# Hybrid decoder step on one core: transposed outputs and norm sums move to the small-work banks, sampled scores go ahead of attention, hosted work starts later

## The reference

```python
u = rmsnorm(h, norm_mix_g);  proj = u @ w_in
oa = banded_attention(...)            # A: window 128, 4 q heads, 2 kv heads, sinks
ob = ssd_chunked(...)                 # B: Mamba-2 scan in 16 chunks of 128
oc = dilated attention                # C: (128,1), (512,4), (2048,16), joined per query
h = h + concat(oa, ob, oc) @ w_out
u2 = rmsnorm(h, norm_mlp_g)
h = h + square(relu(u2 @ w_up)) @ w_down      # w_up 1024 x 4096, w_down 4096 x 1024
```

## Time and profile before

| | |
|---|---|
| median of 3 runs | 2558.17 us (2557.70 to 2562.37) |
| the profiled execution, its own time | 2557.03 us |
| span in its profile | 2554.8 us, 43225 instructions |
| TensorE busy | 2410.4 us, 94% |
| VectorE, ScalarE, GpSimd busy | 48%, 33%, 11% |
| granted TensorE clock, mean | 0.98 of full speed |
| DMA | 414 MB, 162 GB/s |

### The profile page before, as it was taken

How to read it: one execution, slowest core, us unless ns; L and a number is a source line. 1 busy time by engine, 2 the same in 40 slices (tenths; PEclk the granted TensorE clock), 3 DMA queues, 4 the chain that set the end, 5 groups by cost and what they waited for, 6 DMA issues and landing times.

```text
span 2554.8 us, 43225 instructions
## 1 busy us (share of the span) xinstructions
PE 2410.4 (94%) x17509; PEld 1411.2 (55%) x17509; DVE 1234.8 (48%) x2843; ACT 846.2 (33%) x1533; POOL 278.7 (11%) x305
## 2 busy tenths in 40 slices
PE   7899968999888999999899999989999999999999
PEld 4455535555434555444455554445655447788887
DVE  3445446566646767742644654135566521422222
ACT  4444235464435443331433331124432111311210
POOL 0111222111102211001110100011101001000000
PEclk8899989999999999999999999999999999999999
DMA  6454264665574667775434556533455553322232
GB/s 209 166 173 165 100 229 150 215 209 181 177 237 154 213 204 230 246 257 180 154 118 153 153 163 178 159 119 106 156 172 167 159 163 117 96 92 99 93 99 81
DMA packets 327588, 414.44 MB, mean 162 GB/s; under 512 B 62111, under 2 KB 248095, under 8 KB 327136
## 3 DMA queue, kind: packets, MB, share of 16 engines
q1 hardware_dynamic: 327392, 411.69, 50.0%
HBM read 300.00 MB, written 111.62 MB: 161 GB/s over the span
## 4 chain that ended last, share of the span: by engine, by line
PE 74%; DVE 6%; ACT 3%; issue 2%; DMA 1%; SPq 1%; POOL 0%; DVEq 0%; ACTq 0%; POOLq 0%
PE core_dense L2299 64%; PE core_spare L2399 2%; PE core_spare L2413 1%; PE core_spare L2387 1%; PE core_spare L2425 1%; PE core_spare L2553 1%; DVE core_col L2013 1%; DVE core_p L1939 1%; ACT core_p L1715 1%; PE core_spare L2547 1%; PE core_spare L2531 0%; PE core_spare L2539 0%; DVE core_h L1907 0%; PE core_spare L2533 0%; DVE core_r L1895 0%
## 5 line engine op out<-in xcount | busy, mean ns | idle before, releaser
L2299 PE MATMUL core_dense<-core_u,core_ring 128*128 128x512 f16 (+2 forms) x4800 | 870.2, 342 | 22.2 <-ACT core_yt L1688 5.7
L2299 PEld LDWEIGHTS core_dense<-core_u,core_ring 128*128 128x128 f16 x4800 | 469.4, 98 | 396.4 <-issue 41.0
L2299 PE MATMUL core_dense<-core_r_hi,core_ring 128*128 128x512 f16 (+2 forms) x2560 | 649.0, 339 | 2.7 <-DVE core_h L1907 1.5
L2299 PE MATMUL core_dense<-core_r_lo,core_ring 128*128 128x512 f16 (+2 forms) x1280 | 434.0, 339 | 0.0
L2299 PEld LDWEIGHTS core_dense<-core_r_hi,core_ring 128*128 128x128 f16 x2560 | 250.4, 98 | 197.9 <-issue 5.7
L2299 PE MATMUL core_dense<-tok_u,core_ring 128*128 128x512 f16 x1152 | 266.0, 387 | 16.8 <-DMA core_ring<-scratch_kept_w 16.8
L1680 ACT ACTIVATE core_r<-core_dense 128x512 f32<-128x512 f32 (+2 forms) x160 | 82.3, 515 | 528.9 <-PE core_dense L2299 528.9
L1895 DVE TENSOR_TENSOR core_r<-core_r 128x512 f32<-128x512 f32 (+2 forms) x160 | 96.4, 603 | 321.6 <-ACT core_r L1680 321.2
L628 PE MATMUL tok_prod<-tok_w_hi,tok_u 128*128 128x512 f16 (+1 forms) x768 | 200.4, 351 | 0.0
L2299 PEld LDWEIGHTS core_dense<-tok_u,core_ring 128*128 128x128 f16 x1152 | 114.0, 100 | 147.7 <-DMA core_ring<-scratch_kept_w 14.3
L2299 PEld LDWEIGHTS core_dense<-core_r_lo,core_ring 128*128 128x128 f16 x1280 | 125.2, 98 | 93.4 <-issue 0.7
(11 more groups left out here) (309 smaller groups left out, 2704.3 us busy)
## 6 DMA issues: line engine op xcount, KB each, us to landing
core_ring<-scratch_kept_w SPq DMA_DIRECT2D x264, 512.0 KB, 4.3
scratch_kept_w<-core_ring SPq DMA_DIRECT2D x72, 512.0 KB, 5.6
core_qkv<-out_tok SPq DMA_DIRECT2D x48, 384.0 KB, 5.6
core_staged<-in_w_up SPq DMA_DIRECT2D x32, 512.0 KB, 4.7
core_staged<-in_w_down SPq DMA_DIRECT2D x32, 512.0 KB, 4.6
out_tok<-tok_tok SPq DMA_DIRECT2D x16, 644.0 KB, 3.0
core_piece<-in_c_kt SPq DMA_DIRECT2D x32, 288.0 KB, 3.9
core_piece<-in_c_v SPq DMA_DIRECT2D x16, 576.0 KB, 4.6
```

Of the source, the lines that this page charges most:

```text
L2299: ins = pe.matmul(bank, w[:, k, part, :], s, start=first and j == 0, stop=last and j == 2, skip_group_check=True)
```

## The change

Three things are done.

1. `y` and `tail` units leave the dense banks: they take spare4 (i even) and spare5 (i odd). `sum` takes spare2, and spare3 for the second piece of block 3. `out`, `up`, `down` and `col` go on alternating on the two dense banks.
2. `sk` stands ahead of the `att` or `scan` unit of its slot instead of behind it, on every engine. Its banks are spare0 and spare1 in slots with attention (`sk_bank`), spare3 and spare4 behind those; before they were spare5 and spare4 throughout.
3. `HOST_FROM` leaves 1, 1 and 3 slots empty at the start of blocks 0, 1 and 2, and all hosted attention, scan and join work comes that much later. `sq` stays at slot 1 (one attention step earlier in terms of the attention), `split` and `sk` of block 1 stay where they were. In block 2 the `sx` units go from slots 0, 2, 4 to the emptied slots 0, 1, 2, and `split`, `sv`, `se` shift by 3 with the attention.

```diff
@@ -935,6 +935,7 @@
         real_no = list(itertools.accumulate((int(t[3]) for t in att), initial=0))
         kind0_no = list(itertools.accumulate((int(t[3] and t[0] == 0) for t in att), initial=0))
         BIAS_SLOT = (0, 1, 2, 0)
+        HOST_FROM = (1, 1, 3)
         OUT_AFTER = ((), (), (0, 1), (2, 3), (4, 5), (6, 7), (), ())
 
         def att_slots(first, end):
@@ -990,7 +991,7 @@
             for b in range(NB):
                 beside = iter(())
                 if b + 1 < NB:
-                    some = [[s] for s in att_slots(att_end[b + 1], att_end[b + 2])]
+                    some = [[] for _ in range(HOST_FROM[b])] + [[s] for s in att_slots(att_end[b + 1], att_end[b + 2])]
                     for c in range(4 * b + 4, 4 * b + 8):
                         x1, x2, x3 = scan_parts(c)
                         some += [[x1], [], [x2], [x3]]
@@ -1001,14 +1002,14 @@
                         some[1] = some[1] + [("sq", 0, 0, 0)]
                         for k in range(16):
                             some[3 + 3 * k] = some[3 + 3 * k] + [("split", k, 0, 0)]
-                            some[5 + 3 * k] = some[5 + 3 * k] + [("sk", k // 2, k % 2, 0)]
+                            some[5 + 3 * k] = [("sk", k // 2, k % 2, 0)] + some[5 + 3 * k]
                     if b == 2:
                         for k in range(3):
-                            some[2 * k] = some[2 * k] + [("sx", k, 0, 0)]
+                            some[k] = some[k] + [("sx", k, 0, 0)]
                         for k in range(16):
-                            some[8 + 2 * k] = some[8 + 2 * k] + [("split", 16 + k, 0, 0)]
-                            some[9 + 2 * k] = some[9 + 2 * k] + [("sv", k // 2, k % 2, 0)]
-                        some[41] = some[41] + [("se", 0, 0, 0)]
+                            some[11 + 2 * k] = some[11 + 2 * k] + [("split", 16 + k, 0, 0)]
+                            some[12 + 2 * k] = some[12 + 2 * k] + [("sv", k // 2, k % 2, 0)]
+                        some[44] = some[44] + [("se", 0, 0, 0)]
                     beside = iter(some)
                 for q in range(4):
                     for f in range(HF):
@@ -1045,6 +1046,10 @@
         order, bank_of, need, last_use = {}, {}, {}, {}
         counts = collections.Counter()
 
+        def sk_bank(n, j, s):
+
+            return (0 if 5 + 3 * (2 * n + j) < att_end[2 + 1] - att_end[2] + 4 else 3) + s
+
         def claim(key, bank, sem, n):
             if bank in last_use:
                 need.setdefault(key, []).append(last_use[bank])
@@ -1063,16 +1068,21 @@
             if kind in ("out", "sum", "up", "down", "y", "tail"):
                 for q, _, _ in pieces(b) if kind in ("out", "sum", "up", "down") else [(0, 0, 0)]:
                     order[kind, b, i, q] = counts[kind]
-                    bank = counts["dense"] % NDENSE
-                    bank_of[kind, b, i, q] = dense[bank]
                     counts[kind] += 1
-                    counts["dense"] += 1
                     if kind in ("y", "tail"):
                         counts["act" if i % 2 else "dve"] += 1
                         free = (y_act, counts["act"]) if i % 2 else (y_dve, counts["dve"])
                     else:
                         free = ({"out": out_added, "sum": total_log, "up": r_ready, "down": down_added}[kind], counts[kind])
-                    claim((kind, b, i, q), f"dense{bank}", *free)
+                    if kind in ("y", "tail", "sum"):
+                        bank = 2 + q if kind == "sum" else 4 + i % 2
+                        bank_of[kind, b, i, q] = spare[bank]
+                        claim((kind, b, i, q), bank, *free)
+                    else:
+                        bank = counts["dense"] % NDENSE
+                        bank_of[kind, b, i, q] = dense[bank]
+                        counts["dense"] += 1
+                        claim((kind, b, i, q), f"dense{bank}", *free)
                 if kind in ("out", "up", "down"):
                     slot_free.append(({"out": out_done, "up": up_done, "down": down_done}[kind], counts[kind]))
             elif kind == "dt" and b:
@@ -1121,8 +1131,8 @@
             elif kind == "sq":
                 claim(("SQ",), 5, smp_step, LOW_Q)
             elif kind == "sk":
-                for bank in (4, 5):
-                    claim(("SK", b, i), bank, smp_taken, 2 * b + i + 1)
+                for s in range(2):
+                    claim(("SK", b, i), sk_bank(b, i, s), smp_taken, 2 * b + i + 1)
             elif kind == "sx" and b == 0:
                 for bank in (0, 1):
                     claim(("SN",), bank, smp_step, SCORED)
@@ -2212,9 +2222,9 @@
                         dve.wait_ge(smp_done, 2 * n + j + 1)
                         for s in range(2):
                             if j == 0:
-                                dve.tensor_copy(st[:, 2 * s:2 * s + 2, now], spare[5 - s][:, 12:20].rearrange("p (q t) -> p q t", t=DEC_T))
+                                dve.tensor_copy(st[:, 2 * s:2 * s + 2, now], spare[sk_bank(n, j, s)][:, 12:20].rearrange("p (q t) -> p q t", t=DEC_T))
                             last = dve.tensor_copy(st.rearrange("p (k h) t -> p k h t", h=4)[:, 1:4, 2 * j + s, now],
-                                                   spare[5 - s][:, 0:12].rearrange("p (k t) -> p k t", t=DEC_T))
+                                                   spare[sk_bank(n, j, s)][:, 0:12].rearrange("p (k t) -> p k t", t=DEC_T))
                         last.then_inc(smp_taken, 1)
                     elif kind == "sx":
                         softmax(n)
@@ -2571,7 +2581,7 @@
                                 for s in range(2):
                                     rows = slice(HD * s, HD * s + HD)
                                     at = 12 + DEC_T * q
-                                    both(spare[5 - s][:, at:at + DEC_T], lambda l: halves[rows, l, KC * P:], lambda l: qs[rows, l, q, DEC_T * n:DEC_T * n + DEC_T])
+                                    both(spare[sk_bank(n, j, s)][:, at:at + DEC_T], lambda l: halves[rows, l, KC * P:], lambda l: qs[rows, l, q, DEC_T * n:DEC_T * n + DEC_T])
                         for k in range(KC):
                             t0, w = (0, DEC_T) if k == 0 else ((k - 1) % 4, 1)
                             row = 0 if k == 0 else 1 + (k - 1) // 4
@@ -2579,7 +2589,7 @@
                                 rows = slice(HD * s, HD * s + HD)
                                 at = row * DEC_T + t0
                                 q0 = DEC_T * n + t0
-                                last = both(spare[5 - s][:, at:at + w], lambda l: halves[rows, l, k * P:(k + 1) * P], lambda l: qs[rows, l, 2 + j, q0:q0 + w])
+                                last = both(spare[sk_bank(n, j, s)][:, at:at + w], lambda l: halves[rows, l, k * P:(k + 1) * P], lambda l: qs[rows, l, 2 + j, q0:q0 + w])
                         last.then_inc(smp_done, 1)
                     elif kind == "sx" and n == 0:
                         free(pe, "SN")
```

## The result

The changed kernel takes 2517.48 us (median of four runs, 2510.2 to 2521.22) against 2558.49 us before: ratio 0.983, 95% interval 0.981 to 0.986. That is 41 us less where 34.7 were forecast. The time lies in the prediction's whole range of 2516 to 2536. In five more runs it took 2515.28 us, ratio 0.984 (0.982 to 0.986). The profiled execution took 2519.41 us, its span is 2517.3 us.

The account below looks back on a forecast made before the run. TensorE, busy 2410.4 of 2554.8 us, bounds the kernel; only its idle and lower-clock time can shrink. Gains of 10.3 + 15.6 + 8.8 = 34.7 us give a median of 2523.4 us, own range 2518 to 2529, whole range 2516 to 2536.

Parts of the forecast that it names:

- All 7.8 us go: Dense tiles behind `y`, hand-overs and end of block 3: all 21 waits for DVE's draining vanish, 7.8 us gained.
- the 1.05 of the sums: Three `sum` matmuls, each waiting 0.35 us for a dense bank: waits vanish on the new banks, 1.05 us gained.
- part 1: `y`, `tail` and `sum` on their own banks: 10.3 us gained in all.
- The `up` pair: Pair behind `y` 7 in the first two hand-overs: 1.1 of 1.9 us gained each, limited by DVE's norm; 2.2 in all.
- the third hand-over: `up` pair there: TensorE already waits for DVE's norm, so an earlier start only spreads the waits; 0 us gained.
- The end: Tails share spare4 and spare5 with `y` 6 and 7, so `tail` 0 waits for DVE's copy; 0.75 us lost.
- 1.2 us of waiting: S behind `sk` in an `up` slot waits 1.2 us for DVE's copies; new waits in all `sk` slots 1.9 us.
- The clock: Slow tiles: block 1's go, 5.7 us gained; in block 2 one likely stays, 1.3 of 2.9 us gained.
- the clock does not follow: Rival, chance 0.18: slow tiles stay or appear elsewhere, 7.0 us of clock and perhaps 2 more lost; 2530 to 2533 us.
- Behind such a gap none was slow: Block 1: no remaining gap exceeds 1.2 us, and no slow tile followed such gaps, so 5.7 us go.
- Moved work ... 0 us: Work shifted by the empty slots moves its DMAs along, covered by early weight loads and slack for storing; 0 us.
- The softmax's chain: Block 2, up to `sx` 2: a 9.1 us chain leaves TensorE waiting 3.1 instead of 7.1 us; 4.0 gained.

Follow-up runs that it names:

- e7_best: Changed kernel with a fourth empty slot in block 2, `sx` 2 in slot 3, and the tails on spare2 and spare3; 2511.78 us, ratio 0.982 to before.
- e2_sk_ahead: Kernel before with only `sk` moved ahead of attention or scan, on its new banks; 1759.68 us from first sum to end, against 1774.54 before.
- e3_empty_slots: Kernel before with only the empty first slots and the softmax units on them; 1766.87 us from first sum to end, against 1774.54 before.
- e1_banks: Kernel before with only `y`, `tail` and `sum` moved to the spare banks; 2544.49 us, ratio 0.994 to before.

## Why the prediction was right or wrong

The direction, the places and most waits came out as told. The gain came out 6.6 us larger than 34.7, and 2517.48 lies just under the 2518 at which the forecast's own range began. The step that failed most is the price of a removed wait: the prediction counted the idle time of its row (0.44 us for a `y`), and the trace shows 0.60 us from start to start. With it come a slow tile that did not stay, a copy that was ready sooner, and a new wait for moved DVE work that was put at nothing. Step by step:

**"All 7.8 us go" (and the 1.05 of the sums).** The waits went, but each was worth more than its idle time. TensorE's timeline, before and then after:

```profile
1186.56 0.38 PE L2299 MATMUL core_dense<-core_r_hi,core_ring 128*128 128x512 f16 x1
1186.77 0.60 PE L2365 MATMUL core_dense<-core_ident,core_h_more 128*128 128x128 f32 x4
```

```profile
1189.00 0.60 PE L2375 MATMUL core_spare<-core_ident,core_h_more 128*128 128x128 f32 x4
1189.44 10.52 PE L2309 MATMUL core_dense<-core_u,core_ring 128*128 128x512 f16 x48
```

Before, the `y` starts at 1186.77 and the next pair at 1187.81, 1.04 us later; after, 0.44 us later. That is 0.60 us saved, where the row of the wait says 0.44. A matmul of 512 columns is shown with 0.38 us but the next starts 0.21 us behind it; the last 0.16 us of each lie beside the next one, unless that one has to wait. So a removed wait gives back its idle time plus 0.16 us, and the second part shows up as *busy* time that vanishes. Stretch 3 shows it clean: clock 1.00 before and after, yet PE busy fell from 370.46 to 369.20. There the tile behind a `y` of 0.2 us idle starts 0.81 us after it before and 0.44 after, so 0.37 are saved. The Trainium skill, "TensorE: Matmul & The Clock Gate", section "Single matmul latency", gives a warm matmul N/2.4 ns and a constant of some 166 ns on top; the 0.38 against 0.21 us here agree with it. I had this in the rows and didn't use it. 36 removed waits (21 + 3 of part 1, 7 `sk`, 2 turned keys, 3 of the softmax) times 0.16 are 5.8 us, most of the surplus. For the `y` units that is measured; for the 15 others it is an estimate that takes the same 0.16 us.

**The `up` pair.** 1.1 of 1.9 us were to be gained, for DVE's norm. The pair takes 11.36 us now instead of 10.52:

```profile
1228.94 11.36 PE L2309 MATMUL core_dense<-core_u,core_ring 128*128 128x512 f16 x48
```

So 0.84 come back as stalls inside the pair, and 1.2 are gained. Right. In the third hand-over 0 was said: the 1.95 us behind `y` 7 are gone, but the pair waits for DVE's norm six times (five of 0.65 or 0.66, one of 0.51) instead of three. Together 3.92 us were idle and 3.79 are, and with 0.16 for each of two more waits that is 0.2 us lost.

**The end.** 0.75 us was charged for the tails' shared banks. `e7_best` gets 0.4 of it back: the chain starts at TensorE, but a store ends it.

**"1.2 us of waiting" in an `up` slot, 1.9 in all.** S waits 0.81 us at that slot. The copies stand in DVE's list where they were reckoned, but `r_lo` ahead of them took 0.69 us and not the 1.03 of the earlier trace rows, so they end 0.4 us sooner. The slot with P in between has no wait. 0.9 us better, with the 0.16.

**The clock.** 5.7 us in block 1 went, right (17.2 us in `e2_sk_ahead`'s stretch 1). In block 2 one slow tile was to stay; none did, 1.6 us more. That step rested on likeness with one gap, and the runs show that a wait of 3.05 us goes either way. What I did not see at all: part 1 alone loses its whole gain of stretch 1 to the clock. The rival "the clock does not follow" was wrong for the whole change and right for a part of it. "Behind such a gap none was slow" held for the gaps of before and after, and not for `e3_empty_slots`, where one of 0.79 us has a slow tile behind it. The Trainium skill, in the same page's section "A second HAM failure mode: psum-queue depth-cycling", has a kernel that oscillates by frequent short idle times; in `e1_banks` and its repetition slow tiles stand behind waits of 1.2 to 3.4 us. Stretch 1 of after, where no wait is over 0.81 us, has none in seven executions of it and of kernels that share it (453.70 us each time). Whether the cycling through banks has a part in it no run here shows.

**"Moved work ... 0 us".** I priced its DMAs and not its DVE work. One slot later, a scan unit's DVE operations stand ahead of `r_lo` at the last `up` of a quarter, and a `down` waits 1.21 us. With a second wait of 0.19 and the 0.16 of each it costs 1.7 us. The softmax's chain, 9.1 us worked out against 3.1 us of wait, was right to 0.05 us, and part by part: after the pair DVE starts on it 2.0 us later, works 3.5 us to the exponentials, and 3.6 us later the last step ends.

Together: 5.8 + 0.2 + 0.35 + 0.9 + 1.6 - 1.7 = 7.2 us more than forecast, against 6.6 measured. Three small terms are in neither: the second piece of block 3's sum held up a tile by 0.17 us, which is gone (0.3 us gained); `sv` waits for its halves four times for 2.7 us in the profile of after and not three times for 2.3 (0.5 lost); and the third hand-over loses 0.2. With them it is 6.8 us, and 0.2 are left that I can't place.

## What to carry to other kernels

A wait of TensorE is worth the distance from start to start that it adds, not the idle time that its row shows: here 0.16 us more for each `y`, and, if all 36 removed waits are priced so, a seventh of the whole gain. Where work is moved by a slot, go through what each engine does in the slot that it lands in; a list that hosts units of unequal length trades waits as it shifts, and one more shift can take them away. Judge an edit by stretches between fixed marks, and edits that shorten waits by all of them together, since some of their gain is clock that only the last one brings.

## What the runs showed of the hardware

The falls of TensorE's clock in the block stage came back in the second execution of each of the three kernels that were run twice (20.5 us at 1.2 GHz both times, 34.1 both times, and 0 both times), whereas the times ahead of the blocks vary by 8 us with the same code. Shortening waits can add slow stretches: with 4.3 us less idle time in stretch 1, `e1_banks` had 4.3 us more busy time. And behind the same wait of 3.05 us four kernels had no, an early, or a late slow stretch; 8.23 us brought one with the first matmul behind it, and 0.79 us in `e3_empty_slots` had a slow tile behind it as well. What sets the outcome is open. A slow stretch need not cost time: in `e2_sk_ahead` 3.4 us at 1.2 GHz lay where TensorE waits for DVE's norm anyway, and stretch 3 kept its 381.5 us.
